# A ring of eight weight slots, filled from two DMA queues instead of one (hybrid decoder step with 32 experts, one core)

## The chip, the core and the metric

The kernel runs on one core of a Trainium2 chip. The metric is the device time of one execution in microseconds (us). A core has the engines PE (matrix multiply), DVE (vector), ACT (activation), POOL (GpSimd) and SP (sync), and 16 DMA engines. An engine that issues DMAs has a queue of its own in the profile: SP's pieces are in q1 (hardware_dynamic), POOL's DMAs in q0 (software_dynamic), ACT's small bias loads in q10. Times before: 1132.9 us median of 3 runs (1132.62 to 1134.03).

## The reference

One layer of a hybrid decoder for 256 prompt rows and 8 sample rows, width 1024, all in f32. A shared input projection feeds window attention and a recurrent branch; both are normalised, joined, projected and added to x. What takes most of the time is the mixture of experts behind it: 32 experts, 4 chosen per row.

```
def moe(x2d, w_router, b_router, w_gu, b_gu, w_dn, b_dn):
    logits = jnp.einsum('td,de->te', x2d, w_router).astype(jnp.float32) + b_router.astype(jnp.float32)
    top_vals, top_idx = lax.top_k(logits, TOP_K)
    gates = jax.nn.softmax(top_vals, axis=-1).astype(x2d.dtype)
    ...
    def expert_block(args):
        xb, e = args
        h = xb @ w_gu[e] + b_gu[e]
        g = jnp.minimum(h[:, 0::2], SWIGLU_LIMIT)
        up = jnp.clip(h[:, 1::2], -SWIGLU_LIMIT, SWIGLU_LIMIT)
        act = (up + 1.0) * (g * jax.nn.sigmoid(SWIGLU_ALPHA * g))
        return act @ w_dn[e] + b_dn[e]
```

Every expert's weights are read once: 1024 x 2048 (gate and up) and 1024 x 1024 (down) in f32, 12 MB for an expert and 32 experts.

## The kernel before, in words

All five engines run programs written out by hand, which wait on semaphores. The first part (up to about 190 us) is the projection, the attention, the recurrent branch, the output projection and the router, for all 264 rows. The second part goes through the 32 experts in 16 pairs (`pair`, L1567). An expert has room for 64 rows; an expert with more would get further blocks, which this input has not (192 pieces are loaded, 6 for each of 32 experts).

An expert's weights come in 6 pieces (`PIECES`) of 2 MB: four of gate and up (256 rows of the weight each, L1523), two of down (512 rows each, L1549). Each of the 128 partitions gets 16 KB that lie together in HBM. Piece i, counted from 0 over all experts, goes to slot i % 8 (`SLOTS`): slots 0 to 5 are the tensor `ring`, slot 6 is the end of `regA`, slot 7 the start of `regX`. The places of the ring are therefore even or odd as the pieces are: of expert x, pieces 6x, 6x+2 and 6x+4 are even. PE uses the pieces strictly in order; before each it waits for that slot's semaphore (`landed`, L1505), and behind the last matmul of each it raises `m_used`.

All pieces are issued by SP (`load_piece`, L289). The first eight go out during the first part, each when its slot's earlier tenant is no longer needed: pieces 0 to 3 straight behind the projection's weights (L300), 4 and 5 after the attention scratch is free (L315 to L320), 7 and 6 after the router (L325 to L329). Then a loop (L331, seven rounds of 24 pieces, and 16 more behind it) waits for `m_used` to reach n + 1 and loads piece n + 8 into the slot that PE has just left. SP then stores the outputs.

POOL's program in the first part: small loads, two copies of the caches from HBM to HBM, the multiply of the router weights by a gain (L424), the depthwise convolutions (`convolve`, L409), stores of new keys, values and states (L437 to L449), and a memset (L452). In the expert part POOL has no work. DVE and ACT do the activation between gate-up and down, and the adding-up of results; ACT also issues an expert's bias load of two rows twice for each expert (L663).

Of the kernel before, what the change touches and what calls it, by code (L numbers as in the profile page):

```python
# [25 lines left out]
P = 128  # L26
D = 1024
KT = D // P
# [3 lines left out]
NT = 3  # L32
# [5 lines left out]
E = 32  # L38
TK = 4
FF = 1024  # L40
D_IN = 1792
CAP = 64
N_OVER = 16
ITEMS = E + N_OVER
PIECES = 6
GU = 4
SLOTS = 8
# [27 lines left out]
def hybrid_layer(nc, a, o):  # L75

    ctx = ExitStack()
    with ctx:
# [33 lines left out]
        ovi = sb("ovi", [1, 1 + N_OVER], I32)  # L112
# [46 lines left out]
        def chosen(n0, n):  # L159
            return regA[:, 11264 + n0:11264 + n0 + n]  # L160
# [8 lines left out]
        slot = [ring[:, s, :] for s in range(6)] + [regA[:, tail - PIECE:tail], regX[:, 0:PIECE]]  # L169

        def at(x, j):
            return divmod(PIECES * x + j, SLOTS)
# [40 lines left out]
        s_win = [sem(f"win_landed{k}") for k in range(KT)]  # L213
        s_slot = [sem(f"slot_landed{j}") for j in range(SLOTS)]
# [11 lines left out]
        S = {n: sem(n) for n in names}  # L226
        s_kout, s_tok, s_hout, s_cout, s_wout_r = map(sem, ("kv_stored", "tokens_and_bias_landed", "h_stored",
                                                             "conv_stored", "wout_rnn_landed"))
# [10 lines left out]
        w_gu = a["w_gate_up"].rearrange("l e k n -> (l e k) n")  # L239
# [16 lines left out]
            return up  # L256


        @block.sync
        def _(sp):  # L260
            xp = a["x_prompt"].rearrange("b t d -> (b t) d")
            xsm = a["x_sample"].rearrange("b t d -> (b t) d")
            for i in range(2):
                sp.dma_start(x_row[:, i, :], xp[i * P:(i + 1) * P, :]).then_inc(s_x[i], 16)
            sp.dma_start(x_row[0:NS, 2, :], xsm).then_inc(s_x[2], 16)
            sp.dma_start(v0, a["g_mix_norm"].rearrange("l (k p) -> (l k) p", p=P)).then_inc(s_gm, 16)
            sp.dma_start(con[:, :], a["const"][:, :]).then_inc(s_con, 16)

            def load_w_in(k):
                sp.dma_start(w_in[:, k, :], a["w_in"][0, P * k:P * k + P, :]).then_inc(s_win[k], 16)  # L270

            for k in range(4):
                load_w_in(k)
            for r0, n, src in ((R_CONV, 24, a["state_conv"][0].rearrange("b j c -> (b j) c")),
                               (R_H0, NS, a["state_h"][0]), (R_CW, 4, a["conv_w"][0]), (R_CB, 1, a["conv_b"]),
                               (R_BA, 1, a["b_lru_a"].rearrange("l n c -> l (n c)")),
                               (R_BX, 1, a["b_lru_x"].rearrange("l n c -> l (n c)")),
                               (R_LAM, 1, a["lru_lambda"]), (R_GR, 1, a["g_rnn_out"])):
                sp.dma_start(v1[r0:r0 + n, :], src).then_inc(s_vrow, 16)
            for g in range(2):  # L280
                sp.dma_start(v1[R_GA:R_GA + 1, :].rearrange("p (c g d) -> p g c d", g=2, d=HD)[:, g],
                             a["g_attn_out"].rearrange("l (g c d) -> l g c d", g=2, d=HD)[:, g]).then_inc(s_vrow, 16)
                for n, w in enumerate((a["g_q_norm"], a["g_k_norm"])):
                    sp.dma_start(v2[n:n + 1, 64 * g:64 * g + 64], w).then_inc(s_vrow, 16)
            sp.dma_start(v2[2:2 + KT, :], a["g_ffn_norm"].rearrange("l (k p) -> (l k) p", p=P)).then_inc(s_vrow, 16)
            for k in range(4, KT):
                load_w_in(k)

            def load_piece(s, e, j):  # L289
                if j < GU:  # L290
                    src = w_gu[bass.ds(e * D + j * 2 * P, 2 * P), :].rearrange("(p t) n -> p t n", t=2)
                    sp.dma_start(slot[s].rearrange("p (t n) -> p t n", t=2), src).then_inc(s_slot[s], 16)
                else:
                    src = w_dn[bass.ds(e * FF + (j - GU) * 4 * P, 4 * P), :].rearrange("(p t) n -> p t n", t=4)
                    sp.dma_start(slot[s].rearrange("p (t n) -> p t n", t=4), src).then_inc(s_slot[s], 16)

            def load_first(i):
                load_piece(i, i // PIECES, i % PIECES)

            for i in range(4):  # L300
                load_first(i)

            sp.wait_ge(S["proj"], 14)
            for g in range(2):
                sp.dma_start(w_out[64 * g:64 * g + 64, 0:NC, :],
                             a["w_out"][0, 256 * g:256 * g + 256, :].rearrange("(c d) n -> d c n", d=HD)
                             ).then_inc(s_wout, 16)
            sp.dma_start(w_out[:, NC:KT, :],
                         a["w_out"][0, DG:D, :].rearrange("(c p) n -> p c n", p=P)).then_inc(s_wout_r, 16)

            sp.wait_ge(S["kr_tr"], 1)
            sp.wait_ge(S["qbd_r"], 2)
            sp.dma_start(gf_bc, a["g_ffn_norm"].to_broadcast([P, D])).then_inc(s_gf, 16)

            sp.wait_ge(S["pv"], 2)  # L315
            sp.wait_ge(S["ms_o"], 1)
            load_first(4)
            sp.wait_ge(S["s_pv"], 1)
            sp.wait_ge(s_cout, 32)
            load_first(5)  # L320

            sp.wait_ge(S["out_r"], 5)
            sp.dma_start(tokens, a["tokens"][:, :]).then_inc(s_tok, 16)
            sp.dma_start(bias_dn, a["b_down"][0]).then_inc(s_tok, 16)
            sp.wait_ge(S["logit"], NT)  # L325
            load_first(7)
            sp.wait_ge(S["xn"], NT)
            sp.wait_ge(S["st_tr"], 3)
            load_first(6)  # L329

            with sp.Fori(0, E // 4 - 1) as u:  # L331
                for n in range(4 * PIECES):
                    x, j = divmod(SLOTS + n, PIECES)
                    sp.wait_ge(m_used, u * (4 * PIECES) + (n + 1))
                    load_piece(n % SLOTS, u * 4 + x, j)
            for i in range(E * PIECES - 2 * SLOTS, E * PIECES):
                sp.wait_ge(m_used, i - SLOTS + 1)
                load_piece(i % SLOTS, i // PIECES, i % PIECES)
            sp.wait_ge(S["ovd"], 1)
            n_over = sp.value_load(ovi[0:1, 0:1], min_val=0, max_val=N_OVER // 2)  # L340
            with sp.If(n_over > 0):
                with sp.Fori(0, n_over) as m:
                    sp.wait_ge(m_used, m * (2 * PIECES) + E * PIECES)
                    for odd in range(2):
                        e = sp.value_load(ovi[0:1, bass.ds(m * 2 + 1 + odd, 1)], min_val=0, max_val=E - 1)
                        for j in range(PIECES):
                            again, s = at(odd, j)
                            if again:
                                sp.wait_ge(m_used, m * (2 * PIECES) + (E * PIECES + s + 1))
                            load_piece(s, e, j)  # L350

            yp = o["y_prompt"][0]
            done = PAIRS * ADDS
            sp.wait_ge(m_add, ADDS * n_over + (done + 4))
            sp.sem_inc(sp_passed, 1)
            for j in range(4):
                sp.dma_start(o["y_sample"][:, 0, 256 * j:256 * j + 256],
                             xq[32 * j:32 * j + NS, :]).then_inc(s_out, 16)
            for i in range(2):
                sp.wait_ge(m_add, ADDS * n_over + (done + 6 + 2 * i))  # L360
                sp.sem_inc(sp_passed, 1)
                sp.dma_start(yp[P * i:P * i + P, :], x_row[:, i, :]).then_inc(s_out, 16)
            sp.wait_ge(s_out, 16 * 6)
            sp.wait_ge(s_kout, 16 * 7)
            sp.wait_ge(s_hout, 32)
            sp.wait_ge(s_cout, 32)
# [3 lines left out]
        def _(pool):  # L370
# [48 lines left out]
            def per_channel(r):  # L419
# [3 lines left out]
            pool.wait_ge(S["ht_cp"], 9)  # L423
            then(pool.tensor_tensor(wr[:, :, :], wr[:, :, :], vg[:, 2:2 + KT, None].to_broadcast([P, KT, E]), ALU.mult),  # L424
                 "wr_g")
            for c in range(NC):
                convolve(c)
            out = xc[:, :, NP_:T]
            then(pool.tensor_tensor(out, xs[:, :, :], per_channel(R_CW + 3), ALU.mult))
            for j in range(3):  # L430
# [13 lines left out]
            pool.dma_start(o["new_k_prompt"][0, 0].rearrange("w k d -> w (k d)"), k_rows[:, 0, :]).then_inc(s_kout, 16)  # L444
            pool.dma_start(o["new_k_sample"][0, :, 127].rearrange("b k d -> b (k d)"),
                           k_rows[0:NS, 1, :]).then_inc(s_kout, 16)
            pool.wait_ge(S["st_cp"], 3)
            pool.dma_start(o["new_h_prompt"][0], st2[0:1, :]).then_inc(s_hout, 16)
            pool.dma_start(o["new_h_sample"][0], st2[1:9, :]).then_inc(s_hout, 16)  # L449

            pool.wait_ge(S["ms_o"], 2)
            pool.memset(chosen(0, 300), 0.0).then_inc(s_zero, 1)  # L452


        @block.scalar
# [1260 lines left out]
```

## Time and profile before

| | |
|---|---|
| median of 3 runs | 1132.9 us |
| the profiled execution | 1134.25 us |
| its span, first to last instruction | 1132.3 us |
| PE busy | 1076.4 us (95%) |
| DVE, ACT, POOL busy | 323.8, 152.5, 47.9 us |
| q1 (SP's queue) | 418.08 MB, 88.2% of 16 engines' span |
| q0 (POOL's queue) | 2.75 MB, 0.7% |
| chain that ended last | PE 74%, DMA 20%, DVE 2%, ACT 2% |

A busy share is time in which an instruction of that engine ran. The chain is followed back from the last instruction, at each step to what released it. A DMA share of 1 means that all 16 DMA engines moved packets all the time; packets overlap a little, so shares of 1.01 occur. A matmul in f32 is recorded as two matmul instructions, so the 32 matmuls of an expert's gate and up are 64 in the trace, 16 for a piece.

### The profile page before, as it was taken

Reading aid. Unit: us, or ns where it says so; the run is one execution under the profiler, and the core shown is the slowest. Engines: PE = TensorE matmul, PEld = TensorE weight load, DVE = VectorE, ACT = ScalarE, POOL = GpSimd, SP = SyncE. Lnnn points to the kernel's source line nnn. Section 1 sums busy time; section 2 is a strip of 40 time slices with the busy share of each in tenths; the row PEclk is TensorE's granted clock in tenths of the full one; section 3 lists DMA queues with packets and bytes.
Section 4 is the critical chain, followed back from the end, with each engine's and each line's share of the span. In section 5 each row is a group of like instructions: output and inputs, shape, how many; then the busy total and the mean of one; then the engine's idle time right before and its main releaser. Section 6 shows DMA issues by size and latency. Waiting matters only on the chain.

```text
span 1132.3 us, 12759 instructions
## 1 busy us (share of the span) xinstructions
PE 1076.4 (95%) x4945; PEld 428.5 (38%) x4945; DVE 323.8 (29%) x651; ACT 152.5 (13%) x278; POOL 47.9 (4%) x78
## 2 busy tenths in 40 slices
PE   4999987999999999999999999999999999999996
PEld 3676543333333333333333333333333323333332
DVE  1383438413131313131313131313131221213132
ACT  2143512010101010101010101011110101010100
POOL 4154000000000000000000000000000000000000
PEclk9999977899999999999999999999999999999998
DMA  9905404999999999999999999999999999999991
GB/s 338 376 5 147 175 11 150 359 428 418 427 425 430 427 427 427 429 429 427 428 429 430 426 427 429 430 426 428 430 429 427 428 430 428 427 429 427 428 425 73
DMA packets 32684, 421.51 MB, mean 372 GB/s; under 512 B 4386, under 2 KB 4626, under 8 KB 8062
## 3 DMA queue, kind: packets, MB, share of 16 engines
q1 hardware_dynamic: 31134, 418.08, 88.2%
q0 software_dynamic: 1264, 2.75, 0.7%
q8 instruction: 21, 0.34, 0.1%
q10 hardware_dynamic: 256, 0.26, 0.1%
q14 instruction: 9, 0.07, 0.0%
HBM read 419.81 MB, written 2.33 MB: 373 GB/s over the span
## 4 chain that ended last, share of the span: by engine, by line
PE 74%; DMA 20%; DVE 2%; ACT 2%; issue 1%; SPq 0%; DVEq 0%; ACTq 0%
PE ps L1523 29%; DMA ring<-in_w_gate_up_dram 20%; PE ps L1549 16%; PE ps L1483 9%; PE ps L1171 3%; PE ps L1195 3%; PE ps L1565 3%; PE ps L1531 2%; PE ps L1368 1%; PE ps L1198 1%; PE ps L1500 1%; PE ps L1181 1%; DMA con<-in_const_dram 1%; PE ps L1559 0%; PE ps L1269 0%
## 5 line engine op out<-in xcount | busy, mean ns | idle before, releaser
L1523 PE MATMUL ps<-ring,regA 128*64 128x512 f32 x1536 | 339.2, 595 | 15.0 <-DMA ring<-in_w_gate_up_dram 14.6
L1523 PEld LDWEIGHTS ps<-ring,regA 128*64 128x64 f32 x1536 | 109.8, 137 | 238.7 <-issue 208.8
L1549 PE MATMUL ps<-ring,regA 128*64 128x512 f32 x768 | 174.0, 602 | 0.1
L1121 DVE TENSOR_SCALAR regA<-ps 128x512 f32<-128x512 f32 x32 | 22.1, 692 | 415.8 <-PE ps L1531 415.8
L654 ACT ACTIVATE regA<-regA 128x512 f32<-128x512 f32 x32 | 20.1, 630 | 661.1 <-DVE regA L1121 661.1
L1135 DVE COPY regA<-ps 64x512 f32<-64x512 f32 x64 | 44.1, 689 | 206.5 <-PE ps L1549 205.5
L1483 PE MATMUL ps<-regA 128*128 128x512 f32 (+1 forms) x192 | 97.5, 634 | 2.0 <-DVE regA L1044 2.0
L1549 PEld LDWEIGHTS ps<-ring,regA 128*64 128x64 f32 x768 | 53.2, 138 | 107.2 <-issue 97.7
L1565 PE MATMUL ps<-regA 128*128 128x512 f32 (+1 forms) x136 | 66.6, 613 | 0.0
L1523 PE MATMUL ps<-regX,regA 128*64 128x512 f32 x256 | 57.6, 592 | 0.0
L1523 PE MATMUL ps<-regA 128*64 128x512 f32 x256 | 57.6, 592 | 0.0
L1483 PEld LDWEIGHTS ps<-regA 128*128 128x128 f32 (+1 forms) x192 | 31.5, 189 | 67.0 <-issue 64.9
L1115 DVE TENSOR_TENSOR x_row<-x_row,ps 128x512 f32<-128x512 f32 x68 | 42.3, 682 | 1.5 <-PE ps L1565 0.8
L1195 PE MATMUL ps<-regX,regA 128*128 128x264 f32 x160 | 38.8, 392 | 0.0
L1531 PE MATMUL ps<-regA,con 2*64 2x512 f32 x256 | 34.8, 613 | 0.0
L1368 PE MATMUL ps<-regA,regX 128*128 128x512 f32 x64 | 33.4, 676 | 1.2 <-issue 0.7
L1565 PEld LDWEIGHTS ps<-regA 128*128 128x128 f32 (+1 forms) x136 | 23.6, 192 | 24.4 <-issue 24.4
L1195 PEld LDWEIGHTS ps<-regX,regA 128*128 128x128 f32 x160 | 29.4, 190 | 8.0 <-issue 3.5
L1523 PEld LDWEIGHTS ps<-regA 128*64 128x64 f32 x256 | 18.4, 137 | 36.6 <-issue 36.6
L1523 PEld LDWEIGHTS ps<-regX,regA 128*64 128x64 f32 x256 | 18.3, 137 | 36.6 <-issue 34.5
L1549 PE MATMUL ps<-regA 128*64 128x512 f32 x128 | 31.1, 630 | 0.7 <-issue 0.7
L1171 PEld LDWEIGHTS ps<-con,regA 128*128 128x128 f32 (+3 forms) x141 | 20.4, 197 | 24.2 <-issue 12.2
(270 smaller groups left out, 720.3 us busy)
## 6 DMA issues: line engine op xcount, KB each, us to landing
ring<-in_w_gate_up_dram SPq DMA_DIRECT2D x96, 2048.0 KB, 27.9
ring<-in_w_down_dram SPq DMA_DIRECT2D x48, 2048.0 KB, 30.5
regX<-in_w_gate_up_dram SPq DMA_DIRECT2D x16, 2048.0 KB, 26.9
regA<-in_w_gate_up_dram SPq DMA_DIRECT2D x16, 2048.0 KB, 25.7
regA<-in_w_down_dram SPq DMA_DIRECT2D x8, 2048.0 KB, 30.7
regX<-in_w_down_dram SPq DMA_DIRECT2D x8, 2048.0 KB, 32.1
regA<-in_w_in_dram SPq DMA_DIRECT2D x8, 896.0 KB, 14.3
regA<-in_w_out_dram SPq DMA_DIRECT2D x2, 1024.0 KB, 10.5
```

What stands on the lines that cost most here:

```text
L654: act.activation(sig_sb, g_sb, ACT.Sigmoid, scale=ALPHA).then_inc(m_sig, 1)
L1115: dve.tensor_tensor(half, half, ps[:, PLACE[i][h], :], ALU.add).then_inc(m_add, 1)
L1121: dve.tensor_scalar(g_sb, gu[:, 0::2], LIMIT, None, ALU.min).then_inc(m_g, 1)
L1135: dve.tensor_copy(y_sb[n][64 * odd:64 * odd + 64, :], ps[64 * n:64 * n + 64, 4, :]).then_inc(m_ysb, 1)
L1171: return pe.transpose(out, in_, ident[0:k, 0:k])
L1195: return pe.matmul(ps[:, bank, 0:T], w_in[:, kt, P * n:P * n + P], hT[:, kt, :], start=(kt == 0), stop=(kt == KT - 1))
L1368: mm = pe.matmul(ps[:, bank, :], src[:, c, P * i:P * i + P], w_out[:, NC * half + c, 512 * n:512 * n + 512], start=(c == 0), stop=(c == NC ...
L1483: mm = pe.matmul(ps[:, 5 * half, :], oneh[r, i, :], xn_row[r, i, 512 * half:512 * half + 512], start=(i == 0), stop=(i == NT - 1))
L1523: mm = pe.matmul(ps[64 * h:64 * h + 64, 1 + n, :], xT[:, kt, 64 * odd:64 * odd + 64], w[:, c:c + 512], start=(kt == 0), stop=False)
L1531: mm = pe.matmul(ps[64 * h:64 * h + 64, 1 + n, :], selb[32 * n:32 * n + 2, h, :], b_gu[odd][32 * n:32 * n + 2, :], start=False, stop=True)
L1549: mm = pe.matmul(ps[64 * n:64 * n + 64, 4, :], actT[:, j, 64 * h:64 * h + 64], w[:, 1024 * j + 512 * n:1024 * j + 512 * n + 512], start=(h ...
L1565: return pe.matmul(ps[:, PLACE[i][h], :], lhs[:, P * i:P * i + P], rhs[h], start=True, stop=True)
```

## The change

`load_piece` takes the queue as an argument and moves out of SP's program, and a new function `rest_of_pieces(q, mine)` holds the loop of refills and loads only the pieces of one parity. SP calls it for the even places and POOL for the odd ones. Both loops wait for the same counts of `m_used` as before. Of the first eight pieces POOL takes 1 and 3 (after the last projection weights have landed, behind the router multiply), 5 (with the waits that SP had before it) and 7. SP keeps 0, 2, 4 and 6. Nothing else changes: sizes, slots, PE's order and its waits are the same.

```diff
+        def load_piece(q, s, e, j):
+            if j < GU:
+                src = w_gu[bass.ds(e * D + j * 2 * P, 2 * P), :].rearrange("(p t) n -> p t n", t=2)
+                q.dma_start(slot[s].rearrange("p (t n) -> p t n", t=2), src).then_inc(s_slot[s], 16)
+            else:
...
+        def rest_of_pieces(q, mine):
+
+            with q.Fori(0, E // 4 - 1) as u:
+                for n in range(4 * PIECES):
+                    x, j = divmod(SLOTS + n, PIECES)
+                    if n % 2 == mine:
+                        q.wait_ge(m_used, u * (4 * PIECES) + (n + 1))
+                        load_piece(q, n % SLOTS, u * 4 + x, j)
+            for i in range(E * PIECES - 2 * SLOTS, E * PIECES):
+                if i % 2 == mine:
+                    q.wait_ge(m_used, i - SLOTS + 1)
+                    load_piece(q, i % SLOTS, i // PIECES, i % PIECES)
...
-            for i in range(4):
+            for i in (0, 2):
                 load_first(i)
...
             load_first(4)
-            sp.wait_ge(S["s_pv"], 1)
-            sp.wait_ge(s_cout, 32)
-            load_first(5)
...
             sp.wait_ge(S["logit"], NT)
-            load_first(7)
...
+            n_over = rest_of_pieces(sp, 0)
...
+            pool.wait_ge(s_win[KT - 1], 16)
+            for i in (1, 3):
+                load_piece(pool, i, i // PIECES, i % PIECES)
             for c in range(NC):
                 convolve(c)
...
+            pool.wait_ge(S["pv"], 2)
+            pool.wait_ge(S["ms_o"], 1)
+            pool.wait_ge(S["s_pv"], 1)
+            pool.wait_ge(s_cout, 32)
+            load_piece(pool, 5, 0, 5)
             pool.wait_ge(S["st_cp"], 3)
...
             pool.memset(chosen(0, 300), 0.0).then_inc(s_zero, 1)
+            pool.wait_ge(S["logit"], NT)
+            load_piece(pool, 7, 1, 1)
+            rest_of_pieces(pool, 1)
```

How the instructions stand on two engines. The lines of the changed kernel are other ones (`load_piece` is L262 and L265 there, the loop L269).

POOL's program between the router multiply and the first convolution, before:

```order
L424 TENSOR_TENSOR wr<-wr,vecg 128x256
L413 TENSOR_SCALAR regX<-regA,vecg 128x256
L416 TENSOR_SCALAR tap<-regA,vecg 128x256
L417 TENSOR_TENSOR regX<-regX,tap 128x256
L416 TENSOR_SCALAR tap<-regA,vecg 128x256
```

and changed:

```order
L428 TENSOR_TENSOR wr<-wr,vecg 128x256
L262 DMA ring<-in_w_gate_up_dram 128x4096 x2
L417 TENSOR_SCALAR regX<-regA,vecg 128x256
L420 TENSOR_SCALAR tap<-regA,vecg 128x256
L421 TENSOR_TENSOR regX<-regX,tap 128x256
```

Pieces 1 and 3 now stand between the two.

POOL's program from the store of the new keys to its end, before:

```order
L444 DMA out_new_k_prompt_dram<-vT 128x128
L445 DMA out_new_k_sample_dram<-vT 8x128
L448 DMA out_new_h_prompt_dram<-x_row 16x1x32
L449 DMA out_new_h_sample_dram<-x_row 8x512
L452 MEMSET regA 128x300
L78 UNCONDITIONAL_BRANCH
```

and changed, up to the second refill of its loop:

```order
L451 DMA out_new_k_prompt_dram<-vT 128x128
L452 DMA out_new_k_sample_dram<-vT 8x128
L265 DMA ring<-in_w_down_dram 128x4096
L460 DMA out_new_h_prompt_dram<-x_row 16x1x32
L461 DMA out_new_h_sample_dram<-x_row 8x512
L464 MEMSET regA 128x300
L262 DMA regX<-in_w_gate_up_dram 128x4096
L269 UNCONDITIONAL_BRANCH
L269 ISA
L262 ISA
L262 DMA ring<-in_w_gate_up_dram 128x4096
L273 REGISTER_ALU
```

Piece 5 stands ahead of the state stores (h is the recurrent state), piece 7 behind the memset, and then the loop begins.

SP's loop, its first refills, before (ISA is the wait for `m_used`):

```order
L331 ISA
L292 ISA
L292 DMA ring<-in_w_gate_up_dram 128x4096
L334 REGISTER_ALU
L292 ISA
L292 DMA ring<-in_w_gate_up_dram 128x4096
L334 REGISTER_ALU
L295 ISA
L295 DMA ring<-in_w_down_dram 128x4096
```

and changed:

```order
L269 ISA
L262 ISA
L262 DMA ring<-in_w_gate_up_dram 128x4096
L273 REGISTER_ALU
L265 ISA
L265 DMA ring<-in_w_down_dram 128x4096
L273 REGISTER_ALU
```

Every second refill is gone from SP; it stands in POOL's loop.

## Rows read from the trace of the kernel before

**Rows 1.** The page: the span, and busy tenths in 40 slices.

```profile
span 1132.3 us, 12759 instructions
...
PE   4999987999999999999999999999999999999996
...
DMA  9905404999999999999999999999999999999991
GB/s 338 376 5 147 175 11 150 359 428 418 427 425 430 427 427 427 429 429 427 428 429 430 426 427 429 430 426 428 430 429 427 428 430 428 427 429 427 428 425 73
```

**Rows 2.** The chain of waits in order of time: start us, us, what.

```profile
192.07 15.46 PE ps L1523 x64
...
310.98 13.73 PE ps L1523 x64
...
367.73 13.73 PE ps L1523 x64
...
715.61 31.85 DMA ring<-in_w_gate_up_dram
...
806.91 3.65 PE ps L1523 x16
...
866.30 3.65 PE ps L1523 x16
```

**Rows 3.** Who waited for whom: us in total, times, longest us.

```profile
PE ps L1523 <- DMA ring<-in_w_gate_up_dram: 14.6, 14, 1.2
```

**Rows 4.** The timeline of PE from 1098 us: start us, us.

```profile
1098.66 3.65 PE L1523 MATMUL ps<-ring,regA 128*64 128x512 f32 x16 [0.58 <-DMA ring<-in_w_gate_up_dram]
1103.55 3.65 PE L1523 MATMUL ps<-ring,regA 128*64 128x512 f32 x16 [1.24 <-DMA ring<-in_w_gate_up_dram]
...
1113.02 5.48 PE L1549 MATMUL ps<-regA 128*64 128x512 f32 x16 [0.73 <-issue]
```

**Rows 5.** The table by stretches.

```profile
core 0: us, PE busy (x) PEld busy (x) DVE busy (x) ACT busy (x) POOL busy (x), PEclk, DMA share, GB/s
56.00:85.00 29.00, 27.05 (x158) 22.08 (x157) 23.78 (x51) 12.81 (x51) 16.57 (x20) 0.94 0.02 7
...
806.90:866.30 59.40, 57.27 (x258) 20.19 (x258) 13.71 (x25) 6.02 (x9) 0.00 (x0) 1.00 1.01 428
1103.50:1108.50 5.00, 4.67 (x24) 1.26 (x24) 0.21 (x1) 0.00 (x0) 0.00 (x0) 1.00 0.49 210
1108.50:1113.40 4.90, 1.51 (x6) 1.05 (x8) 2.47 (x4) 1.23 (x2) 0.00 (x0) 0.64 0.05 20
```

**Rows 6.** The timeline of POOL; in brackets the idle time before.

```profile
23.10 0.56 POOL L391 DMA_DIRECT2D brt<-in_b_router_dram  x1
...
58.52 0.63 POOL L413 TENSOR_SCALAR regX<-regA,vecg 128x256 f32<-128x256 f32 x1 [7.86 <-ACT regA L500]
...
146.36 0.52 POOL L448 DMA_DIRECT2D out_new_h_prompt_dram<-x_row  x1 [44.99 <-ACT x_row L597]
```

**Rows 7.** The timeline of SP: one refill.

```profile
692.14 0.33 SPq L295 DMA_DIRECT2D ring<-in_w_down_dram  x1
```

**Rows 8.** The DMA queues from 40 to 50 us: packets, MB, share of 16 engines.

```profile
q1 hardware_dynamic: 287, 4.18, 98.3%
q0 software_dynamic: 287, 0.02, 2.0%
```

**Rows 9.** The DMA queues from 1000 to 1060 us.

```profile
q1 hardware_dynamic: 1757, 25.63, 100.4%
```

**Rows 10.** The DMA queues from 50 to 60 us.

```profile
q0 software_dynamic: 170, 1.09, 26.1%
q1 hardware_dynamic: 76, 0.98, 23.6%
```

More of the change, by code:

```diff
@@ L256, in counter @@
             return up
+        def load_piece(q, s, e, j):
[3 more added lines that the diff above has]
+            else:
+                src = w_dn[bass.ds(e * FF + (j - GU) * 4 * P, 4 * P), :].rearrange("(p t) n -> p t n", t=4)
+                q.dma_start(slot[s].rearrange("p (t n) -> p t n", t=4), src).then_inc(s_slot[s], 16)
+        def rest_of_pieces(q, mine):
[9 more added lines that the diff above has]
+                    load_piece(q, i % SLOTS, i // PIECES, i % PIECES)
+            q.wait_ge(S["ovd"], 1)
+            n_over = q.value_load(ovi[0:1, 0:1], min_val=0, max_val=N_OVER // 2)
+            with q.If(n_over > 0):
+                with q.Fori(0, n_over) as m:
+                    q.wait_ge(m_used, m * (2 * PIECES) + E * PIECES)
+                    for odd in range(2):
+                        e = q.value_load(ovi[0:1, bass.ds(m * 2 + 1 + odd, 1)], min_val=0, max_val=E - 1)
+                        for j in range(PIECES):
+                            again, s = at(odd, j)
+                            if s % 2 == mine:
+                                if again:
+                                    q.wait_ge(m_used, m * (2 * PIECES) + (E * PIECES + s + 1))
+                                load_piece(q, s, e, j)
+            return n_over
         @block.sync
@@ L287, in _ @@
                 load_w_in(k)
[L289 to L295, printed above, removed]
             def load_first(i):
-                load_piece(i, i // PIECES, i % PIECES)
-            for i in range(4):
+                load_piece(sp, i, i // PIECES, i % PIECES)
+            for i in (0, 2):
                 load_first(i)
@@ L329, in _ @@
             load_first(6)
[L331 to L350, printed above, removed]
+            n_over = rest_of_pieces(sp, 0)
             yp = o["y_prompt"][0]
```

## The prediction

> **What bounds the kernel now.** I read the page's 40 slices first [rows 1]. PE is at 9 or more nearly everywhere, but so is DMA from slice 8 on, at 425 to 430 GB/s. Two resources look full at once, and the slices cannot say which one ends last. The table by stretches and the chain of waits can. An expert pair (12 pieces of 2 MB) takes PE 56.75 us early on: its first gate-up run starts at 310.98 us and the next pair's at 367.73, with no DMA between. From 715 us on the chain has a DMA step in every pair: a piece issued at 715.61 us lands 31.85 us later, and PE goes on the moment it lands. There the pairs are 59.39 us apart (806.91, 866.30) [rows 2]. So PE is the faster by 2.6 us a pair; it lives on the eight full slots until they are used up, and then DMA sets the pace at 59.4 / 12 = 4.95 us a piece. The view of waits agrees: PE waited for the ring 14 times, 14.6 us in all, never over 1.2 us [rows 3]. That 14.6 us is all that any faster delivery can win.
>
> One more thing is to be seen at the end. The last piece PE waits for is piece 189 (the fourth gate-up piece of expert 31, an odd place): it starts at 1103.55 us [rows 4], and 28.75 us later the span ends. Between 1103.5 and 1108.5 us the DMA share is already 0.49, then 0.05, which is about one engine in sixteen (0.06) [rows 5]. Most engines are done, and one trails. Hence the pace: 12 pieces are 25.17 MB, at the 428 GB/s of the stretch 58.8 us, and yet a pair takes 59.4. The last two pieces follow at 4.95 us each, so transfers end at 1103.5 + 9.9 = 1113.4 us.
>
> **The change part by part.**
>
> *Early loads.* Pieces 1 and 3 go from SP to POOL, behind the router multiply. POOL then stands idle 7.86 us for ACT, until its first convolution at 58.52 us [rows 6]. A POOL issue of 128 rows takes 0.56 us [rows 6], one on SP 0.33 [rows 7]: two are 1.1 us and lie inside that gap. The transfers move into a stretch in which DMA is 2% busy (56 to 85 us) [rows 5], and PE reads them only after 192 us [rows 2]. Cost 0; without the gap it would be 1.1 us of convolution. Piece 5 goes to POOL between the key stores and the recurrent-state stores, where POOL idles 44.99 us [rows 6]; behind it are only those two stores and one memset. Piece 7 comes after the memset, when POOL has no work left. All four are full long before PE starts on the experts. Cost 0.
>
> *Issue of the 184 refills.* 92 go to each queue. POOL takes 0.2 us longer for one. A piece waits some 30 us behind others (31.85 us from issue to landing, of which 4.95 is its own transfer), so 0.2 us is hidden while the queues are full. Cost 0, and 0.2 us if the queue were empty.
>
> *Rate of the engines.* The kernel before never moved 16 KB rows on POOL's queue, so I bound this. For two queues at once, the stretch 40 to 50 us has 287 packets of each, one for one, although POOL's were tiny (0.02 MB) [rows 8]. SP's moved 4.18 MB in 98.3% of 16 x 10 us, 26.6 GB/s an engine; alone, in 1000 to 1060 us, it is 25.63 MB in 100.4% of 16 x 60 us, the same 26.6 [rows 9]. Alternating costs nothing. For POOL's own packets, in 50 to 60 us they moved 1.09 MB in 26.1%, 26.1 GB/s an engine, beside SP's 0.98 MB in 23.6%, 26.0 [rows 10]. I take no change of rate, because the only rows with large POOL packets (the cache copies, HBM to HBM) lie beside SP's to 1%. Upper end: 26.1 against 26.6 is 2% on half of the pieces, 92 x 4.95 x 0.02 = +9 us. Lower end: -9 us, from the trailing engine (rival 3).
>
> *Order of landing.* This is the term that is left. One queue lands piece n whole before n+1 gets a byte. Two queues that share packet for packet (287 to 287) carry n and n+1 together. If n+1 has a part f done when n lands, n is late by f x 4.95 us; n+1 then lands with 1 - f of n+2 done, late by (1 - f) x 4.95. The two delays sum to 4.95 us. While DMA sets the pace a constant lag costs nothing per pair, for the engines are never idle; it is paid once, where the stream ends. The last wait is for 189, an odd place, so the end moves by the odd lag, 0 to 4.95 us. Pieces are freed 3.4 us (as one is used) to 4.9 us (PE waiting) apart, so SP has a head start of a part of a piece, and the odd ones carry some of the lag but hardly all: PE waits before 188 too (0.58 us, beside 1.24 before 189) [rows 4]. I take the middle, **+2.5 us**. Piece 191 still lands by 1113.4 us, when PE starts on piece 190, so it adds nothing.
>
> Sum: 0 + 0 + 0 + 2.5 us. The profiled execution took 1134.25 us with a span of 1132.3; the median of the runs is 1132.9. I add to the median: **1135.4 us**, and the span would be about 1134.8. A measurement of this kernel can tell about 0.2%, 2.3 us, from no change.
>
> **The rivals.**
>
> 1. *One queue falls behind.* Shares need not be equal for 900 us. Four pieces of 92 are 4%, so a share of 48% is enough for one queue to be its whole four slots late at the end. The other then runs dry, and the last pieces of the late one run alone. If POOL is late, 187 lands 9.9 us before the end of the transfers, at 1103.5; PE needs 3 x 3.43 = 10.3 us (3.43 is a quarter of the 13.73 us of a run [rows 2]) for 187 to 189, to 1113.8 instead of 1107.2: +6.6. If SP is late, 188 lands at 1108.5, and PE is through 189 at 1115.4: +8.2. Time 1139.5 to 1141.1. Against it: 287 to 287.
>
> 2. *GpSimd's copies are slower on some engine.* A piece has landed when its slowest engine has, and one engine trails already. With the 2% above the time is 1135.4 + 9 = 1144.4 us; it decides from about 0.1% on. For it: the 2%. Against it: SP's own packets were as slow in that stretch. The Trainium skill, page "DMA: Bandwidth & Descriptors", section "Latency and other measured facts", says that engines 7 and 15 are usually slower, by its best guess because the descriptor rings of GpSimd's copies lie behind the same ports. By that rule this is what happens to every odd piece; no row of this trace tells the engines apart, and the one that trails does so with no GpSimd copy in sight.
>
> 3. *Not slower: the trailing engine is relieved.* Its pace, not the 428 GB/s, sets 59.4 us. If work in two queues spreads its extra load, a pair falls to 58.8, or 0.05 us for each of 184 pieces: 1135.4 - 9.2 = 1126.2 us, and never below 1132.9 - 14.6 = 1118.3. It decides once a pair is under 59.2 us (-2.5 over some 15 pairs). Against it: both queues put each partition's row through the same sixteen engines as far as the packets show, and a full engine gains nothing from a second queue.
>
> 4. *Side by side in name only.* If the two queues take turns by whole pieces the landings stay as they are: 1132.9 us. Against it again the one-for-one packets.
>
> **How the numbers follow.** My case 0.56, with its own range 1132.9 to 1137.9 (lag 0 to 4.95 us); the lag is under 2.3 us in a little less than half of it: 0.26 same, 0.30 slower. Rival 1 has 0.12, all slower; rival 2 0.13, of which 0.10 slower and 0.03 too small to tell; rival 3 0.14, faster; rival 4 0.05, same. That makes 0.14 faster, 0.34 same, 0.52 slower. The range runs from 1130.0, which leaves out most of rival 3, to 1146.0, which takes in rivals 1 and 2.
>
> **What would show it.** Right: POOL's queue carries half of the bytes, the stretches stay at 427 to 429 GB/s, the pairs stay 59.4 us apart late, PE's first wait for the ring comes some pairs sooner, the issue-to-landing time stays near 30 us on both queues, and 189 is used 1 to 4 us after 1103.55. Wrong on the rate: late pairs at 58.8 or at 60 us. Wrong on the shares: landing times far apart between the queues, and one of them silent in the last 20 us. Wrong on the early part: the first gate-up product does not start near 192 us.

## The result and the profile after

| | before | after |
|---|---|---|
| median | 1133.99 us (1132.42 to 1136.16, 17 runs) | 1138.03 us (1135.87 to 1139.53, 17 runs) |
| the profiled execution | 1134.25 us, span 1132.3 | 1139.43 us, span 1137.7 |
| PE waits for gate-up pieces in `ring` | 14.6 us, 14 times | 17.2 us, 17 times |
| pairs, late | 59.39 us apart | 59.38 us apart |
| piece 189 used, from the start of the experts | 911.48 us | 914.71 us |

The changed kernel is slower: ratio 1.0036, 95% interval [1.0029, 1.0043], so 3.3 to 4.9 us. The start of the experts is the first gate-up run of the chain (192.07 before [rows 2], 193.84 after). I count from it below, because it lies anywhere from 190.67 to 193.84 in the profiled executions whose starts are given here.

The page of the changed kernel: queues (packets, MB, share of 16 engines), and pieces by queue with the median us from issue to landing.

```profile
span 1137.7 us, 12782 instructions
...
q1 hardware_dynamic: 17310, 216.74, 45.9%
q0 software_dynamic: 15088, 204.08, 42.6%
...
ring<-in_w_gate_up_dram SPq DMA_DIRECT2D x48, 2048.0 KB, 28.5
ring<-in_w_gate_up_dram POOLq DMA_DIRECT2D x48, 2048.0 KB, 28.6
```

The bytes are halved between the queues and neither queue is behind. The DMA queues from 1000 to 1060 us show how evenly:

```profile
q0 software_dynamic: 879, 12.83, 50.3%
q1 hardware_dynamic: 878, 12.81, 50.1%
```

Together that is 25.64 MB where SP's queue alone had 25.63 [rows 9]. The table by stretches has the same rate, 428 GB/s, in the middle; what differs is the end [rows 5]:

```profile
core 0: us, PE busy (x) PEld busy (x) DVE busy (x) ACT busy (x) POOL busy (x), PEclk, DMA share, GB/s
...
806.90:866.30 59.40, 57.27 (x258) 20.19 (x258) 13.71 (x25) 6.01 (x9) 3.17 (x7) 1.00 1.01 428
1103.50:1108.50 5.00, 3.65 (x16) 1.06 (x16) 0.00 (x0) 0.00 (x0) 0.00 (x0) 1.00 0.85 360
1108.50:1113.40 4.90, 4.67 (x24) 1.26 (x24) 0.11 (x1) 0.00 (x0) 0.00 (x0) 1.00 0.13 54
```

PE's timeline at the end, beside [rows 4]:

```profile
1103.67 3.65 PE L1538 MATMUL ps<-ring,regA 128*64 128x512 f32 x16 [0.60 <-DMA ring<-in_w_gate_up_dram]
1108.55 3.65 PE L1538 MATMUL ps<-ring,regA 128*64 128x512 f32 x16 [1.23 <-DMA ring<-in_w_gate_up_dram]
```

The two waits have their old lengths, 0.6 and 1.2 us; they only come later. Piece 188 is used 3.2 us later than before, counted from the start of the experts, just as 189 is. The chain shows that PE reads the first pieces at 193.84, and that its first DMA step comes two pairs before the one at 715.61 [rows 2]:

```profile
193.84 15.44 PE ps L1538 x64
...
604.21 29.63 DMA ring<-in_w_gate_up_dram
...
661.72 31.48 DMA ring<-in_w_gate_up_dram
```

The profiled executions differ by 5.4 us of span: 1.77 in the start of the experts, 3.23 in the use of 189 counted from there, 0.4 behind it. Nothing ties the 1.77 to the change. PE's granted clock was 0.66 in 75 to 85 us here and 1.00 before; and in the profiles of the runs below the experts begin at 190.67 to 192.42 where GpSimd loads early pieces (runs 1, 3, 4, 5 and 7), and at 191.02 to 193.75 where it loads none (runs 2, 6, 11 and 12).

The last piece of all, 191, can be followed from its issue to its landing. Before, changed, and run 12 below (the timeline's line of the issue, then, from the view of DMAs asked for that issue alone, the us from issue to landing):

```profile
1078.54 0.33 SPq L295 DMA_DIRECT2D regX<-in_w_down_dram  x1
regX<-in_w_down_dram SPq DMA_DIRECT2D x1, 2048.0 KB, 34.6
...
1083.81 0.54 POOL L265 DMA_DIRECT2D regX<-in_w_down_dram  x1 [6.33 <-PE ps L1538]
regX<-in_w_down_dram POOLq DMA_DIRECT2D x1, 2048.0 KB, 31.9
...
1085.69 0.54 POOL L266 DMA_DIRECT2D regX<-in_w_down_dram  x1 [6.45 <-PE ps L1540]
regX<-in_w_down_dram POOLq DMA_DIRECT2D x1, 2048.0 KB, 28.9
```

From the start of the experts it lands at 921.1, 921.9 and 920.8 us. So in the changed kernel the stream as a whole ends only 0.8 us later, while 188 and 189 are 3.2 us late: the other 2.4 us are order of landing. The account behind the runs uses this.

### The profile page after: what moved, and what is told of

The parts are those of the page before. It is cut to its first block, busy times and chain, and to the rows that moved or that the text cites. A ratio compares the mean times of both kernels' runs of the same rounds, so it can differ in the third digit from the quotient of the medians.

```text
span 1137.7 us, 12782 instructions
## 1 busy us (share of the span) xinstructions
PE 1078.2 (95%) x4945; PEld 430.0 (38%) x4945; DVE 323.5 (28%) x651; ACT 152.5 (13%) x278; POOL 99.6 (9%) x175
## 4 chain that ended last, share of the span: by engine, by line
PE 68%; DMA 25%; DVE 2%; ACT 2%; issue 1%; SPq 0%; DVEq 0%; POOLq 0%; ACTq 0%
PE ps L1538 25%; DMA ring<-in_w_gate_up_dram 25%; PE ps L1564 15%; PE ps L1498 8%; PE ps L1210 4%; PE ps L1186 3%; PE ps L1580 3%; PE ps L1546 2%; PE ps L1213 2%; PE ps L1383 1%; PE ps L1515 1%; PE ps L1196 1%; DMA con<-in_const_dram 1%; PE ps L1284 0%; PE ps L1574 0%
## 5 line engine op out<-in xcount | busy, mean ns | idle before, releaser
L1538 PE MATMUL ps<-ring,regA 128*64 128x512 f32 x1536 | 339.7, 596 | 17.6 <-DMA ring<-in_w_gate_up_dram 17.2
L262 POOL DMA_DIRECT2D ring<-in_w_gate_up_dram x48 | 25.9, 540 | 483.0 <-PE ps L1564 315.3
L1210 PE MATMUL ps<-regX,regA 128*128 128x264 f32 x160 | 41.6, 414 | 0.0
L1383 PE MATMUL ps<-regA,regX 128*128 128x512 f32 x64 | 31.0, 635 | 1.8 <-ACT regX L607 1.0
## 6 DMA issues: line engine op xcount, KB each, us to landing
ring<-in_w_gate_up_dram SPq DMA_DIRECT2D x48, 2048.0 KB, 28.5
ring<-in_w_gate_up_dram POOLq DMA_DIRECT2D x48, 2048.0 KB, 28.6
regX<-in_w_gate_up_dram POOLq DMA_DIRECT2D x16, 2048.0 KB, 28.5
```

What stands on the lines that cost most here:

```text
L262: q.dma_start(slot[s].rearrange("p (t n) -> p t n", t=2), src).then_inc(s_slot[s], 16)
L1210: return pe.matmul(ps[:, bank, 0:T], w_in[:, kt, P * n:P * n + P], hT[:, kt, :], start=(kt == 0), stop=(kt == KT - 1))
L1383: mm = pe.matmul(ps[:, bank, :], src[:, c, P * i:P * i + P], w_out[:, NC * half + c, 512 * n:512 * n + 512], start=(c == 0), stop=(c == NC ...
L1538: mm = pe.matmul(ps[64 * h:64 * h + 64, 1 + n, :], xT[:, kt, 64 * odd:64 * odd + 64], w[:, c:c + 512], start=(kt == 0), stop=False)
```

## The experiments

Theory A is the prediction's: pieces that travel side by side land late by a constant lag, paid once. All ratios are to the kernel before in runs on the same chip, with 95% intervals. Where a slot is filled now from one queue and now from the other, a run counts some of the landings on semaphores of their own, and gives up two that nothing waits for; the excerpts below don't show that.

**1. The early pieces alone.** The first eight as in the changed kernel, every refill on SP:

```diff
-            rest_of_pieces(pool, 1)
...
-                    if n % 2 == mine:
+                    if True:
```

> Only the early part of the change: POOL loads pieces 1, 3, 5 and 7, SP all 184 refills. Theory A (order of landing: the lag of the odd pieces is paid once at the end): same as before within 0.2%, last gate-up run at 1103 to 1104 us plus whatever the start of the experts moves. Theory B (the early loads on POOL delay the first part by the 1.8 us by which the experts started later in the changed kernel): +1.8 us, start of the experts at 193.8. Theory C (GpSimd's copies are slower on the engines): same as before.

1135.01 us, ratio 1.0007 [0.9998, 1.0015]. Experts begin at 191.04, 189 is used 911.36 us later; PE's waits are 14.5 us, 14 times. The early part costs nothing that can be told from noise (-0.2 to 1.7 us).

**2. The refills alone.** The first eight on SP as before, the refills split as in the changed kernel:

```diff
-            for i in (0, 2):
+            for i in range(4):
                 load_first(i)
...
-            load_piece(pool, 7, 1, 1)
```

> Only the refills of the change: SP loads the first eight pieces as before, the 184 refills are split odd and even. Theory A: +2.3 to +3.3 us, and the first waits of PE for the ring two pairs sooner than before. Theory B: 4.0 less 1.8, so about +2.2, with the experts starting at 192.1. Theory C: +2 to +4 and late pairs over 59.4 us.

1137.0 us, ratio 1.0032 [1.002, 1.0044], +2.3 to +5.0 us: the refills carry the cost. Start 191.02, 189 used 915.26 us later.

**3. The last eight on SP.**

```diff
-                if i % 2 == mine:
+                last = i >= E * PIECES - SLOTS
+                if (0 if last else i % 2) == mine:
```

> The changed kernel, but the last eight pieces (184 to 191) all on SP's queue, one behind the other. Theory A: piece 189 lands two piece times (9.9 us) before the end of the transfers again, so the lag is gone: +0 to +1.8 us against before (the 1.8 only if theory B holds too), 2.3 to 3.3 less than the changed kernel, although 92 - 4 pieces still go by POOL. Theory C: stays at +3.5 to +4 us.

1137.33 us, ratio 1.0027 [1.0016, 1.0038]. A miss: the lag should have gone. PE's timeline (experts from 190.67) says why it had to stay:

```profile
1046.80 5.35 PE L1543 MATMUL ps<-ring,regA 128*64 128x512 f32 x16 [2.42 <-DMA ring<-in_w_gate_up_dram]
...
1095.03 13.90 PE L1543 MATMUL ps<-ring,regA 128*64 128x512 f32 x64
```

The first line is piece 177, used 856.1 us after the start where the kernel before uses it at 852.4 (1044.51 in its timeline). From there PE never waits again: all four pieces 186 to 189 run as one block. PE needs 56.75 us for a pair and DMA 59.4, so PE can win back only some 2.6 us in the last pair, and it was 3.7 us late at 177 and lost 1.7 more on 177 itself, which took 5.35 us in place of 3.65. The last eight pieces, 184 to 191, were in order and landed only 0.6 us later than before; the time had been lost ahead of them.

**4. Two pieces to a queue in turn** (the first eight likewise).

```diff
-                    if n % 2 == mine:
+                    if n // 2 % 2 == mine:
```

> Two pieces to a queue in turn (0 and 1 to SP, 2 and 3 to POOL, 4 and 5 to SP and so on), so pieces n and n+2 go side by side. Theory A: the lag of 189 is one whole piece time instead of a half, +4.9 us against before, +2.5 against the changed kernel; PE's first wait for the ring a pair sooner than in the changed kernel. Theory C: as the changed kernel, for POOL carries just as many pieces.

1141.31 us, ratio 1.0066 [1.0053, 1.0079], +7.5 us. More disorder costs more, as A says. 189 is used 917.84 us after the start (1108.90 after 191.06), 6.4 later than before. Piece 191 lands 1.5 us later than before, so 4.8 of the 6.4 are order, the whole piece that A expected; the 1.5 of the stream were not in its sum.

**5. The last 24 on SP.**

```diff
-                if i % 2 == mine:
+                last = i >= E * PIECES - 3 * SLOTS
+                if (0 if last else i % 2) == mine:
```

> As the changed kernel, but the last 24 pieces (168 to 191) all come from SP's queue, in order; the pieces before them stay split. In the run with only the last eight on SP the lag was already in TensorE's schedule at piece 177 (used 3.7 us later, counted from the start of the experts, than in the kernel before), and from there TensorE ran without a wait to the end, so that test came too late. Theory A (order of landing, paid once, where the last waits lie): with order restored from 168 on, piece 177 is used within 0.5 us of where it is used before (852.4 us after the start of the experts) and 189 within 0.5 us of 911.5; time 0.0 to 1.0 us above before, ratio 1.000 to 1.001. Rival B (every split stretch loses a little of the transfers' time, so the cost grows with the number of split pieces): 160 of 184 refills are still split, the cost is 7/8 of the 3.5 us, so +2.5 to +3.5 us, and the two uses come 2.5 to 3.5 us late.

1135.45 us, ratio 1.0008 [0.9997, 1.0018]. B, which expected at least 2.5 us (1.0022), falls. In the profile 189 is used at 1104.20, 911.78 us after the start 192.42, 0.3 us later than before and within A's 0.5. Piece 191 lands 0.3 us late too, so nothing is left of the order at the end. 177 goes without a wait, some 0.9 us late and not 0.5, because PE had been kept back one pair earlier (piece 165 was used 3.5 us late).

**6. Only the last 24 split.** The complement; the loop ahead of them and the first eight are SP's.

```diff
-                if i % 2 == mine:
+                last = i >= E * PIECES - 3 * SLOTS
+                if (i % 2 if last else 0) == mine:
```

> The complement: everything on SP as in the kernel before, and only the odd ones of the last 24 pieces (168 to 191) on GpSimd's queue. Theory A: the whole cost is there, +2.5 to +4.0 us, ratio 1.002 to 1.0035, and piece 189 is used 2.5 to 4 us later after the start of the experts than before (911.5). Rival B: an eighth of it, +0.2 to +0.7 us.

1144.1 us, ratio 1.0084 [1.007, 1.0098], +9.5 us. Against B (0.2 to 0.7) it is clear; A's own number (2.5 to 4.0) was missed by 5.5 us or more. PE's timeline, and the page's pieces by queue:

```profile
925.40 3.65 PE L1537 MATMUL ps<-ring,regA 128*64 128x512 f32 x16 [1.24 <-DMA ring<-in_w_gate_up_dram]
983.55 5.23 PE L1537 MATMUL ps<-ring,regA 128*64 128x512 f32 x16 [4.52 <-DMA ring<-in_w_gate_up_dram]
993.34 5.35 PE L1537 MATMUL ps<-ring,regA 128*64 128x512 f32 x16 [4.56 <-DMA ring<-in_w_gate_up_dram]
...
1108.03 7.09 PE L1537 MATMUL ps<-ring,regA 128*64 128x512 f32 x32 [1.98 <-DMA ring<-in_w_gate_up_dram]
```

```profile
ring<-in_w_gate_up_dram SPq DMA_DIRECT2D x90, 2048.0 KB, 26.6
...
ring<-in_w_gate_up_dram POOLq DMA_DIRECT2D x6, 2048.0 KB, 17.5
```

Pieces 164 and 165 (983.55 and 993.34) still came from SP's queue, and are late by 3.6 and 8.5 us from the start of the experts (191.78). GpSimd's queue was empty, so its pieces, 169 and on, began at once while older ones of SP's were still in line: they land 17.5 us after their issue, SP's after 26.6 (medians of the whole run). SP's pieces stay behind to the end: 188 (1108.03) is used 9.7 us late, while the last transfer ends 921.0 us after the start, as before (921.1). This is order of landing at its worst. Where both queues have an equal backlog, as in the changed kernel, the lag is smaller.

**7. All refills on GpSimd's queue.** SP's call of `rest_of_pieces` goes.

```diff
-                    if n % 2 == mine:
+                    if mine:
```

> All 184 refills on GpSimd's queue, in order, none on SP's; the first eight pieces as in the changed kernel. One queue, but the software one. Theory A: order of landing is the kernel before's again, so 0.0 to +1.0 us; pair stalls where they are before, and 189 used within 1 us of 911.5 after the start of the experts. Rival C (what GpSimd issues is late or slow in itself: 0.54 against 0.33 us an issue, or a longer way to the engines): twice as many pieces bear it as in the changed kernel, so +4 us or more, with every used place refilled late.

1133.8 us, ratio 0.9994 [0.9984, 1.0003]; 189 used 912.19 us after the start (1103.52 after 191.33), 0.7 later than before and within A's 1. C falls. In the page the 94 pieces to `ring` from POOL have 539 ns an issue:

```profile
L263 POOL DMA_DIRECT2D ring<-in_w_gate_up_dram x94 | 50.6, 539 | 457.1 <-PE ps L1569 290.3
...
ring<-in_w_gate_up_dram POOLq DMA_DIRECT2D x94, 2048.0 KB, 27.5
```

The issue is 0.2 us longer than SP's 0.33 [rows 7], and the landing is 27.5 us after it, no worse than SP's.

**8. Halves by partitions.** Each piece by two transfers, 0 to 63 from SP and 64 to 127 from GpSimd:

```diff
+            h = slice(64, 128) if q is nc.gpsimd else slice(0, 64)
...
+                q.dma_start(slot[s][h].rearrange("p (t n) -> p t n", t=2), src).then_inc(done, 16)
```

> Two queues, but every piece cut in halves by partitions: SP loads partitions 0 to 63 of all 192 pieces and GpSimd 64 to 127 of all 192, so that both queues work on the same piece and pieces land in order. Theory A: 0.0 to +1.0 us, with the lag gone. Rival D (two queues side by side cost something whatever the order: another queue's packets between, two completions to wait for): +2.5 to +4 us as the changed kernel.

1655 us median, from 1615 to 1851 over six runs; the profiled one was the longest, with a span of 1849.4. Neither theory expected that, and it says nothing on order: the transfers themselves were slow, 240 GB/s with the engines full (stretch 700 to 760 us):

```profile
700.00:760.00 60.00, 36.23 (x140) 11.62 (x140) 8.85 (x16) 1.23 (x2) 3.05 (x6) 0.89 1.01 240
```

**9. The same halves, both on SP**, as one edit to the kernel before.

```diff
+                for h in (slice(0, 64), slice(64, 128)):
...
+                        sp.dma_start(slot[s][h].rearrange("p (t n) -> p t n", t=2), src).then_inc(s_slot[s], 16)
```

> The kernel before with one edit: each piece is loaded by two transfers of 64 partitions each (0 to 63, then 64 to 127), both from SP's queue. It asks what halved the rate in the run with halves by partitions. If it was the form (64 partitions in a transfer), this runs at about 240 GB/s and takes 1600 to 1900 us. If it was two queues working at once on the two halves of one piece, this stays within 10 us of the kernel before, at 428 GB/s and 0.615 us a packet.

2030.9 us, ratio 1.790 [1.787, 1.794], slower yet than expected. The form of the transfer halves the rate, for there is no second queue here; the stretch and the queues from 1000 to 1060 us:

```profile
806.90:866.30 59.40, 40.83 (x136) 13.02 (x134) 4.86 (x9) 4.79 (x7) 0.00 (x0) 0.82 1.00 213
```

```profile
q1 hardware_dynamic: 976, 12.78, 100.5%
```

The engines are busy all the time and move 213 GB/s. The Trainium skill, page "SBUF — State Buffer", section "Door 1: The DMA port swizzle (why `[64,N]` ≈ `[32,N]`)", says that bandwidth depends on how many of 16 ports the partitions reach, and that one bit (+64) picks the odd or the even half of them. By that rule 64 partitions below or above the middle get half the rate, and the 213 against 428 here agrees. Why run 8, with a lower and an upper half under way at once, moved no more than 240 the runs don't show.

**10. Halves by columns.** As 8, but each half goes to all 128 partitions, in 8 KB rows (h is 0 on SP, 1 on GpSimd).

```diff
+                q.dma_start(slot[s].rearrange("p (t n) -> p t n", t=2)[:, h:h + 1, :], src).then_inc(done, 16)
```

> Two queues on the same piece again, but cut along its columns, so that each half goes to all 128 partitions: SP loads the first 8 KB of every partition's 16 KB of each piece, GpSimd the second 8 KB; pieces land in order. The halves by partitions had not tested the order, since their 16 KB packets took 1.10 us each in place of 0.615 and the ring fell to 240 GB/s. Theory A (order of landing): with 428 GB/s in the stretch 806.9 to 866.3 as before, the time is 0.0 to +1.0 us. Rival D (two queues side by side cost something whatever the order): 428 GB/s and still +2.5 to +4 us. If the smaller packets move less than 428 GB/s, every pair of experts grows in proportion, the run tells the two apart only by that rate, and 1% of rate is some 8 us.

1148.78 us, ratio 1.0128 [1.0113, 1.0144]. The rate fell a little, so it has to be read by the rate. The stretch, and PE two pairs apart:

```profile
806.90:866.30 59.40, 56.45 (x256) 20.14 (x254) 13.71 (x25) 6.01 (x9) 6.13 (x12) 1.00 1.01 421
```

```profile
755.03 3.65 PE L1551 MATMUL ps<-ring,regA 128*64 128x512 f32 x16 [1.40 <-DMA ring<-in_w_gate_up_dram]
...
875.59 3.65 PE L1551 MATMUL ps<-ring,regA 128*64 128x512 f32 x16 [1.42 <-DMA ring<-in_w_gate_up_dram]
```

A pair takes 60.28 us, 0.89 more than 59.39; over 184 refills, 12 to a pair, that is 13.6 us. 189 is used at 1116.26, 924.93 us after the start (191.33), 13.45 later than before. The rate explains it and leaves no room for D's 2.5 to 4 us. That the rows and not the two queues lower the rate is read from the queues from 1000 to 1060 us: here 12.63 MB in 50.7% of 16 x 60 us on GpSimd's, 25.9 GB/s an engine, where the changed kernel with its two queues has 12.83 MB in 50.3%, 26.6. No run had 8 KB rows on one queue.

**11. The bias loads on GpSimd's queue**, as one edit to the kernel before (ACT's calls of `bias_gu` go).

```diff
+            with pool.Fori(0, PAIRS - 1) as p:
+                for odd in range(2):
+                    pool.wait_ge(m_gu, p * 2 + (odd + 1))
+                    bias_gu(odd, p * 2 + (odd + 2))
```

> The kernel before with one edit: the experts' bias loads (4 KB in packets of 4 bytes, two a load) go from ScalarE's queue to GpSimd's. It tests the prediction's rival of a relieved engine from another side: the ring moves 428 GB/s with the 16 engines 101% busy, and a pair of experts takes 59.4 us where its 24 MB of pieces in packets of 0.613 us alone would need 58.8. If the small packets on one engine are what sets the pair's time, and the other queue spreads them, pairs fall to 58.8 to 59.1 us and the time by 3 to 8 us (1126 to 1131). If not, the pairs stay at 59.4 and the time within 1 us of the kernel before.

1134.02 us, ratio 0.9995 [0.9986, 1.0004]; pairs 59.40 us apart (808.07, 867.47). The expectation has their packets wrong: in the kernel before, q10 has 16 packets and 0.02 MB from 1000 to 1060 us, so they are not packets of 4 bytes alone. The bias loads are not what makes a pair 59.4 and not 58.8. What else does is open, and no version here beats the kernel before.

**12. The split from piece 24 on.** In the profiles where GpSimd has refills from the first on, the engines moved slightly less in the first 120 us of the experts; before, after, run 7 (experts from 191.33), and this run (experts from 193.75):

```profile
192.07:312.07 120.00, 120.00 (x522) 41.78 (x524) 36.21 (x79) 13.53 (x20) 0.00 (x0) 0.96 0.93 387
```

```profile
193.84:313.84 120.00, 120.00 (x522) 41.81 (x524) 36.28 (x79) 13.52 (x20) 6.35 (x12) 0.96 0.93 385
```

```profile
191.33:311.33 120.00, 120.00 (x523) 41.76 (x525) 36.35 (x79) 13.52 (x20) 12.83 (x24) 0.96 0.92 385
```

```profile
193.75:313.75 120.00, 120.00 (x522) 41.78 (x524) 33.40 (x71) 13.52 (x20) 2.08 (x4) 0.96 0.93 388
```

```diff
+            if mine == 0:
+                for i in range(SLOTS, 3 * SLOTS):
+                    q.wait_ge(m_used, i - SLOTS + 1)
+                    load_piece(q, i % SLOTS, i // PIECES, i % PIECES, s_first.get(i % SLOTS))
```

> The refills of the changed kernel, but its split begins later: pieces 0 to 23 all come from SP's queue, and only from piece 24 on, when the engines have had a backlog for some 50 us, do the odd ones go to GpSimd's. In every profile with a split from the first refill the engines moved a little less in the first 120 us after the start of the experts (382 to 386 GB/s; 387 to 389 with one queue, SP's or GpSimd's), after that 428 everywhere. Theory A2 (of the 3.2 us by which piece 189 is used later, some 0.6 us is this: two queues that begin empty fill the engines less well; the other 2.6 us is order of landing): the first 120 us are at 387 or 388 GB/s, 189 is used 2.3 to 2.9 us later than before after the start of the experts (913.8 to 914.4), and the time is 2.5 to 3.5 us above before. Rival E (GpSimd's queue loses that much wherever it joins in): 385 or 386, and 189 still 3.0 to 3.5 us late (914.5 to 915.0). Both expect no large cost of the change of queues here, unlike the run that joined GpSimd's queue at piece 168, since TensorE still has full slots: no wait for the ring before some 570 us.

1137.78 us, ratio 1.0037 [1.0025, 1.005]; its end:

```profile
1108.60 3.65 PE L1540 MATMUL ps<-ring,regA 128*64 128x512 f32 x16 [0.33 <-DMA ring<-in_w_gate_up_dram]
```

One premise of the expectation is off: run 7, with one queue, GpSimd's, moves 385 GB/s like the split ones, so the lower rate goes with GpSimd's queue in the first refills and not with the split. The first 120 us came back to 388 GB/s, as A2 said, and yet 189 is used 914.85 us after the start, 3.4 late, as E said. E is not borne out by that, for the stream lost nothing: 191 lands 0.3 us earlier than before. The 3.4 us are order alone. A2 had taken the share that falls on the odd pieces as fixed, and it is not: 188, on SP's queue, lands 0.9 us late here, where it was 3.2 in the changed kernel. As GpSimd's queue joined at a time when PE had full slots, its overtaking cost PE no wait for the ring before 633.99 us.

## Why the prediction was right, and by how much it was off

The forecast was slower by 2.5 us, with a range to 1146.0; measured were 4.0 us, and 1138.0 in that range. The likeliest case is the one that happened. Its own range, 1132.9 to 1137.9, was counted from a median of 1132.9; the kernel before has 1133.99 in the later runs, and the difference of 4.0 lies between its bounds of 0 and 4.95.

*Order of landing, +2.5 us.* Right in mechanism. How much later than before three pieces land, in us from the start of the experts, each landing read as that of 191 was:

| | changed | run 2 | run 12 |
|---|---|---|---|
| 188, even, SP's | 3.2 | 1.4 | 0.9 |
| 189, odd, GpSimd's | 3.2 | 3.8 | 3.4 |
| 191, the end of the stream | 0.8 | 0.1 | -0.3 |
| 188 less 191: order, even | 2.4 | 1.2 | 1.2 |
| 189 less 191: order, odd | 2.4 | 3.6 | 3.6 |

Before rounding the two delays by order sum to 4.9 us in each, one piece's transfer, as the prediction said. How they share it differs: half and half in the changed kernel's profile, a quarter and three quarters in the other two. What sets the share the runs don't show, so the middle of the bounds was a choice without a row behind it, and that the profiled execution came so near to it is luck. The cause is shown by taking it apart as well: refills in one queue leave the time as it was, whichever queue it is (runs 1 and 7), order restored early enough gives the time back (run 5), and more disorder costs more (runs 4 and 6).

One sentence of the prediction is too strong. That one queue lands a piece whole before the next gets a byte does not go with [rows 5]: after 1103.5 us, when 189 had landed, only some 1.15 MB were moved (5.0 us at 210 GB/s and 4.9 at 20) of the 4.19 MB of pieces 190 and 191. What holds is that pieces land one after another, 4.9 us apart [rows 4], which is enough for the sum.

*The stream itself, put at 0.* The sum had no term for it, and this is the part that was missing. 191 lands 0.8 us late in the changed kernel, and 0.1 to 1.5 in the five runs in which GpSimd has refills from the first on (2 to 5, split, and 7, not split, with 0.7); where it has none in the first 24 pieces it is -0.3 to 0.3 (runs 1, 6, 11 and 12, by the last landing). It goes with the slightly lower rate in the first 120 us, 385 or 386 GB/s for 387 or 388, and so with GpSimd's queue at the start rather than with the split. Why is not shown, and with one profile of each kernel the size is rough. With 2.4 it makes the 3.2 us of 189. Over the executions the cost is 4.0 us [3.3, 4.9], and where the remaining 0.8 us lie the runs don't resolve.

*Paid once, where the stream ends.* Right in the sum, since pairs stayed at 59.4 us, but the place was drawn too narrowly. In run 3 the last pieces landed in time and the cost stayed: the payment ends with the last pair at which DMA still holds PE back, since PE can win back only some 2.6 us in a pair. Order restored 8 pieces from the end was too late, 24 was enough; nothing between was run.

*Early loads, 0.* Right (run 1). *Issue, 0.* Right: 0.54 us on POOL, a little below the 0.56 taken from a smaller load, and hidden (run 7).

*Rate of the engines, 0.* Right where the engines are full: 428 GB/s before and after. Rival 2 (1144.4 us) took 2% on GpSimd's copies; with all refills on its queue the time is the same within 0.2% (run 7). The Trainium skill's rule on engines 7 and 15 (page "DMA: Bandwidth & Descriptors", section "Latency and other measured facts") found no support here: run 7, with all the refills on GpSimd's queue, has 0.9994 of the time. No run tells one engine from another.

*Rival 1* (a queue behind): 879 packets to 878, landing after 28.5 and 28.6 us. It did not happen. *Rival 3* (relieved engine): pairs stayed at 59.38. *Rival 4* (side by side in name only): 17 waits for 14, the first two pairs sooner, and both 188 and 189 later than the stream by 2.4 us say that pieces did travel side by side.

## What to carry to other kernels

A second queue gives no bandwidth where the engines are full (428 GB/s either way). What it changes is the order in which pieces land, and a consumer that takes them in order pays for that once, by a part of a piece's transfer: 2.4 to 3.6 of 4.9 us here. So leave it out where one queue keeps the engines full. Sharing each piece between the queues kept the order but cost 13.5 us by its 8 KB rows (run 10), and an empty queue that joined a full one close to the end cost 9.5 us (run 6). To see whether a late piece is late by order or by rate, compare it with the last piece of the stream. And when undoing a cost at the end of a stream, begin ahead of the last place where the consumer still waits, for behind it there may be little slack to win anything back.

## What the runs showed of the hardware that was not expected

- A transfer to 64 partitions (0 to 63 or 64 to 127) ran at 213 GB/s from one queue, and 240 where two queues took a half each (in the longest of six executions); one to all 128 ran at 428, from the same source and in the same 16 KB rows.
- With two queues, 8 KB rows moved 421 GB/s and 16 KB rows 428. One queue was run with 16 KB rows only.
- Two queues shared the engines packet for packet (879 to 878 in 60 us), and yet the share of a piece's delay that fell on either queue was one half in one kernel and a quarter and three quarters in two others.
- One long wait can cost more than two short ones. In run 3 PE waited 2.42 us before piece 177 and its sixteen matmuls then took 5.35 us, at a granted clock of 0.68 in the stretch (a mean between the levels 1.2 and 2.4 GHz, which are 0.5 and 1), where a piece takes 3.65 us after waits of 1.2. It does not follow every such wait: the same run's timeline has one of 2.39 us with 3.65 behind it. What decides it the runs don't show.

```profile
690.44 3.65 PE L1543 MATMUL ps<-ring,regA 128*64 128x512 f32 x16 [2.39 <-DMA ring<-in_w_gate_up_dram]
```

The stretch of piece 177 (us, the engines' busy time, and at the end granted clock, DMA share, GB/s):

```profile
1046.80:1052.10 5.30, 5.30 (x19) 1.46 (x19) 0.00 (x0) 0.00 (x0) 0.00 (x0) 0.68 1.02 433
```
